# Two tables of half-block positions: the first head's steps and the last head's steps move by half a unit

## The chip, the cores and the metric

The kernel runs on one core of one Trainium2 chip. A core has a matrix engine (TensorE, PE in the rows; PEld are its weight loads), a vector engine (VectorE, DVE), an activation engine (ScalarE, ACT), a general engine (GpSimd, POOL) and a queue engine (SyncE, SP) that issues most transfers. The metric is the device time of one execution in microseconds, as the median of three runs.

## The reference

One layer of a decoder with four parallel branches, for 1024 prompt tokens and 8 x 4 sample tokens:

```python
h = rmsnorm(x, norm_g)
p = einsum('btd,dn->btn', h, w_in)        # one projection feeds all branches
o_a = silu(a_z) * (a_b * dwconv3(a_c * a_u))
o_r = silu(r_z) * head_norm(retention_chunked(rq, rk, r_v, S))      # 4 heads
o_c = silu(c_z) * silu(layernorm(dwconv31(glu)))
o_m = silu(m_z) * head_norm(sigmoid(m_o) * mlstm_chunked(q, k, v, i, f, C, n, m))   # 4 heads
proj = einsum('btnw,nwd->btnd', stack(o_a, o_r, o_c, o_m), w_br)
y = x + einsum('btd,de->bte', sum_n sigmoid(g_n) * proj_n, w_out)
```

Both kinds of heads work in chunks of 128 tokens: within a chunk by a masked product of q and k, between chunks by a state that is carried on. The results are the normalised outputs of the prompt and the sample, and the new states.

## The kernel before

Tokens lie along the free axis, channels on the partitions. Every large product is done in three parts (high x high, high x low, low x high), lines 1155 to 1157. The projection is cut into units of 128 output channels. A unit has three blocks of 352 tokens, a block two halves of 12 products each. There are 8 heads: heads 0 to 3 are mLSTM, heads 4 to 7 retention. While PE computes the units of the next head, the small matrix products of the head before are put between its halves.

The order is written out by a planner, `make_plan` (line 74). `phase` (line 78) lays out the halves of a group of units and puts the tasks of a table behind them: a task at position x comes after half x of the phase. `attention` (line 103) gives the 15 steps of a head: eight steps over the prompt's chunks, in which step c does the output of chunk c-1 (`b`) and the transposes and scores of chunk c (`a`); then the last chunk's output with the sample tokens' start (`as`); the sample tokens' products with the first state update (`bs1`) and the head's statistics (`pn`); the second state update (`bs2`); the normalisation (`pr`); an empty step; and the transposes back, first the prompt (`pt 0`), then the sample (`pt 1`). Each engine walks through the same list and does its own part of each entry, in that order, with waits on semaphores.

The places that matter here:

- `a` on PE, lines 1291 to 1312: L1308, L1309 and L1311 transpose k, v and o, L1312 is the score product. For the first head it waits until the gates are done (L2379 on DVE). ACT then makes kw (L1585), the sigmoid of o (L1597) and v (L1598), DVE the weighted scores sw (L2401).
- `b` on PE, L1327 to L1331, needs sw and v.
- `bs1` on PE, L1343 to L1354, ends with the first four state products (L1353, L1354); `bs2` is L1353 and L1354 again and needs DVE's first update (L2438) done.
- `pn` on DVE: L2471, L2474. `pr`: ACT's square root (L1626), DVE's reciprocal and shift (L2480, L2482), ACT's and DVE's scaling (L1629, L2487).
- `pt`: L1367 and L1371 on PE; L1371 waits until DVE has used the first of L1367's two results (L2498).
- In the last head's phase the units are cv, cg, z of that head, and two gate units (positions 0 to 29). The z unit's blocks are evicted by ACT (L1508) and DVE (L2022). Beside the head's steps the phase holds sums for the next stage (`comb`, `comb_split`, `comb4`: L2212, L1689, L1841, and the t4f operations L2224 to L2228, which need the result of L1841).
- The next stage is made of products of 264 tokens (L1204 to L1206). Its P7 product needs DVE's sum (L2073), behind the t4f operations and the first convolution taps (L1715, L2511) in DVE's queue.

Of the kernel before, what the change touches and what calls it, by code (L numbers as in the profile page):

```python
# [73 lines left out]
def make_plan():  # L74
# [3 lines left out]
    def phase(group, tasks):  # L78

        first, at = len(units), 0  # L80
        units.extend(group)
        blocks = [(u, b) for u in range(first, len(units)) for b in range(3)]
        if not first:

            blocks[:9] = [(u, b) for b in range(3) for u in range(3)]
        for u, b in blocks:
            for half in range(2):
                plan.append(("blk", u, b, half))
                if b == 2 and half:
                    plan.append(("unit_end", u))  # L90
                plan.extend(tasks.pop(at, ()))
                at += 1
        for more in sorted(tasks):
            plan.extend(tasks[more])

    def spread(steps, start, stride):

        out = {}
        for i, s in enumerate(steps):
            out.setdefault(int(start + i * stride), []).extend(s)  # L100
        return out

    def attention(hd):
        t = [[("a", hd, 0)]]
        t += [[("b", hd, c - 1), ("a", hd, c)] for c in range(1, CH)]
        t += [[("b", hd, CH - 1), ("as", hd)], [("bs1", hd), ("pn", hd)], [("bs2", hd)],
              [("pr", hd)], [], [("pt", hd, 0)], [("pt", hd, 1)]]
        return t

    def cols(base, h):  # L110
        return ("wa", (base + h * P) // P)

    def mlstm(h):
        return [("mq", cols(5632, h), h), ("mk", cols(6144, h), h), ("mv", cols(6656, h), h), ("mo", cols(7168, h), h)]
# [4 lines left out]
    def z(hd):  # L119
        return [("z", cols(7680, hd) if hd < 4 else cols(3584, hd - 4), hd)]  # L120

    def late(group, late_unit):

        return group[:2] + late_unit + group[2:]
# [8 lines left out]
    phase([("if", ("wi", 0), 0)] + mlstm(0)[:2] + z(0) + mlstm(0)[2:], gates)  # L133
    for h in range(1, 4):
        if h == 1:
            phase(mlstm(1), {x: step for x, step in zip((1, 3, 5, 6, 8, 9, 11, 12, 14, 15, 16, 17, 19, 21, 22), attention(0))})
        else:
            phase(late(mlstm(h), z(h - 1)), spread(attention(h - 1), 0, 2.05))
    for h in range(4):
# [10 lines left out]
        phase(late(ret(h), z(h + 3)), tasks)  # L150

    tasks = {}
    for x, step in zip((0, 1, 2, 4, 5, 6, 8, 9, 11, 13, 15, 16, 17, 18, 19), attention(7)):
        tasks.setdefault(x, []).extend(step)
    for i in range(6):
        tasks.setdefault(2 * i + 1, []).append(("comb", 3, i))
# [197 lines left out]
    for m in range(len(outs)):  # L354
        for b in range(3):
            plan_out.append(("pblk", m, b))
            x = 3 * m + b
# [16 lines left out]


UNITS, PAIRS, OUTS, SPL, LOADS, START, PLAN, SLOT_OF, PREV, AT_LOAD, AT_SPLIT, LAST_RING = make_plan()
NU, NW, NSPL = len(UNITS), len(PAIRS), len(SPL)
BRANCH_LAST = [8 * i + 7 for i in range(4)]
# [2359 lines left out]
```

How the kernel before makes its waits and increments, by code:

```python
        def loaded(eng, item):  # L920
            slot, n = LOADED[AT_LOAD[item]]
            eng.wait_ge(w_in[slot], 16 * n)
            return stage[slot]
# [1 line left out]
        def low_parts(eng, s):  # L926
            eng.wait_ge(lo_dve if by_vector(SPL[s]) else lo_done, LOW[s])
# [52 lines left out]
            def wait(self):  # L981
                self.eng.wait_ge(self.s, self.n)
# [2 lines left out]
        @block.sync  # L985
# [9 lines left out]
            def by_token(b):  # L995
                if b == 2:
                    sp.wait_ge(sq_done, 3)
                for j in range(3):
                    r0 = BLK * b + P * j
                    sp.dma_start(xk[b % 2][0:XCH[j], j, :], xtok[r0:r0 + XCH[j], :]).then_inc(xk_in[3 * b + j], 16)
# [14 lines left out]
            load(2, 0)  # L1016
            by_channel(3)
            by_token(2)
            by_channel(4)
            by_channel(5)
            sp.dma_start(vc[:, :, :], vec).then_inc(const_in, 16)
            sp.dma_start(m0t[:, :], m0).then_inc(const_in, 16)
            sp.dma_start(gb[:, :], gbias).then_inc(const_in, 16)
            load(3, 1)
            load(4, 2)
            sp.wait_ge(row_ready, 3)
            sp.dma_start(cst2[:, :], c2).then_inc(late_in, 16)
            def blk(u, b, half):
                if half and UNITS[u][0] == "g":
                    x = GN[(u, b)]
                    sp.wait_ge(freed["A"], FREED[("blk", u, b)][1])
                    sp.dma_start(g_rows[UNITS[u][2], :, tok(b)], gp[x % 2][:, :]).then_inc(gp_out[x % 2], 16)
# [52 lines left out]
        @block.tensor  # L1087
# [16 lines left out]
            pe.wait_ge(ones_set, 1)
            keep_busy(24)
```

## Time and profile before

| what | value |
|---|---|
| median of three runs | 1479.52 us (1478.79 to 1479.61) |
| the profiled execution | 1478.4 us |
| its span, first to last instruction | 1476.6 us |
| mean granted TensorE clock | 0.998 |
| PE busy | 1458.7 us (99%) |
| DVE, POOL, ACT busy | 914.5, 580.5, 520.1 us |

PE is the engine that sets the time. Busy time on the others matters where PE waits for them. The stretches of interest are the first head's first steps (about 95 to 102 us), its sample steps (137 to 140 us), the last head (570 to 592 us) and the start of the next stage (611 to 622 us). In a row of the timeline stand start, length, engine, line, operation, output and inputs, shapes, count, and in brackets the idle time before it with what ended it; start and length are in microseconds from the start of the span.

### The profile page before, as it was taken

The numbers are of one execution on the slowest core, as the hardware profiler recorded it, in microseconds if no ns is written. First come the engines' busy times: TensorE is split into PE (matmuls) and PEld (weight loads), VectorE is DVE, ScalarE is ACT, GpSimd is POOL, SyncE is SP. The second block draws the span as 40 slices with busy tenths as digits, with TensorE's granted clock in tenths as the row PEclk, the third lists the DMA queues.
The fourth block names the chain that finished last, engine by engine and source line by source line (L and its number), as shares of the span: only waits on it lengthen the run. The fifth ranks groups of instructions, "written<-read, shape, count | busy, mean of one in ns | idle before, by whom it ended". The sixth has DMA issues, their size and how long they took to land.

```text
span 1476.6 us, 26706 instructions
## 1 busy us (share of the span) xinstructions
PE 1458.7 (99%) x10318; PEld 1420.6 (96%) x10318; DVE 914.5 (62%) x1786; ACT 520.1 (35%) x1071; POOL 580.5 (39%) x456
## 2 busy tenths in 40 slices
PE   8999999999999999999999999999999999999998
PEld 8999999999999999999999999999999999999786
DVE  6455352556666665677977878867656324885542
ACT  6342333333334345333333342334454422220221
POOL 1000000000011021787777767776777844662100
PEclk9999999999999999999999999999999999999999
DMA  8120222212021121322223221222222476754222
GB/s 316 44 87 29 89 67 80 74 44 91 30 91 62 58 80 50 106 92 91 67 94 95 87 81 68 73 102 88 95 81 102 148 238 207 234 159 149 109 83 78
DMA packets 65527, 148.37 MB, mean 100 GB/s; under 512 B 7976, under 2 KB 36920, under 8 KB 65272
## 3 DMA queue, kind: packets, MB, share of 16 engines
q1 hardware_dynamic: 58008, 120.06, 24.3%
q0 software_dynamic: 6192, 22.27, 4.2%
q10 hardware_dynamic: 1200, 4.33, 0.7%
q8 instruction: 82, 1.34, 0.4%
q14 instruction: 45, 0.37, 0.1%
HBM read 110.99 MB, written 35.64 MB: 99 GB/s over the span
## 4 chain that ended last, share of the span: by engine, by line
PE 88%; DVE 5%; DMA 2%; POOL 2%; issue 1%; ACT 1%; SPq 0%; DVEq 0%; ACTq 0%; POOLq 0%
PE bank L1204 11%; PE bank L1206 11%; PE bank L1205 11%; PE bank L1155 9%; PE bank L1157 9%; PE bank L1156 9%; PE bank L1222 4%; PE bank L1223 4%; PE bank L1224 4%; PE bank L1416 1%; PE bank L1417 1%; PE bank L1418 1%; PE sums_ps L1312 1%; PE sums_ps L1327 1%; PE sums_ps L1331 1%
## 5 line engine op out<-in xcount | busy, mean ns | idle before, releaser
L1155 PE MATMUL bank<-h_hi,w_hi 128*128 128x352 f32 x960 | 319.4, 333 | 1.2 <-POOL w_lo L1802 1.0
L1157 PE MATMUL bank<-h_hi,w_lo 128*128 128x352 f32 x960 | 309.2, 322 | 0.0
L1156 PE MATMUL bank<-h_lo,w_hi 128*128 128x352 f32 x960 | 308.4, 321 | 0.0
L1204 PE MATMUL bank<-h_hi,t_hi 128*128 128x264 f32 x896 | 256.2, 286 | 0.0
L1205 PE MATMUL bank<-h_lo,t_hi 128*128 128x264 f32 x896 | 254.6, 284 | 0.0
L1206 PE MATMUL bank<-h_hi,t_lo 128*128 128x264 f32 x896 | 254.1, 284 | 0.0
L1802 POOL TENSOR_TENSOR t_lo<-stage,t_hi 128x512 fp32r<-128x512 f32 x144 | 194.7, 1355 | 139.5 <-ACT t_hi L1458 139.4
L1204 PE MATMUL bank<-c_hi,t_hi 128*128 128x264 f32 x672 | 191.3, 285 | 2.1 <-DVE part L2073 2.1
L1206 PE MATMUL bank<-c_hi,t_lo 128*128 128x264 f32 x672 | 191.0, 284 | 0.0
L1205 PE MATMUL bank<-c_lo,t_hi 128*128 128x264 f32 x672 | 190.3, 283 | 0.0
L1155 PEld LDWEIGHTS bank<-h_hi,w_hi 128*128 128x128 f32 x960 | 180.5, 188 | 2.9 <-POOL w_lo L1802 1.3
L1156 PEld LDWEIGHTS bank<-h_lo,w_hi 128*128 128x128 f32 x960 | 181.1, 189 | 0.0
L1157 PEld LDWEIGHTS bank<-h_hi,w_lo 128*128 128x128 f32 x960 | 180.3, 188 | 0.0
L1458 ACT ACTIVATE t_hi<-stage 128x512 fp32r<-128x512 f32 x144 | 90.9, 632 | 225.0 <-PE bank L1224 103.4
L1204 PEld LDWEIGHTS bank<-h_hi,t_hi 128*128 128x128 f32 x896 | 168.4, 188 | 0.8 <-issue 0.2
L1205 PEld LDWEIGHTS bank<-h_lo,t_hi 128*128 128x128 f32 x896 | 168.5, 188 | 0.5
L1206 PEld LDWEIGHTS bank<-h_hi,t_lo 128*128 128x128 f32 x896 | 168.5, 188 | 0.0
L2511 DVE SCALAR_TENSOR_TENSOR sums_ps<-ext,vc,sums_ps 128x1024 f32<-128x1024 f32 x116 | 149.1, 1285 | 13.3 <-ACT sums_ps L1715 9.7
L1819 POOL DMA_DIRECT2D out_o_s<-smp x8 | 4.4, 555 | 385.3 <-DVEq L2440 385.3
L1802 POOL TENSOR_TENSOR t_lo<-wsum,t_hi 128x512 fp32r<-128x512 f32 x84 | 111.0, 1323 | 81.2 <-ACT t_hi L1458 81.1
L1204 PEld LDWEIGHTS bank<-c_hi,t_hi 128*128 128x128 f32 x672 | 126.3, 188 | 2.7 <-issue 2.6
L1206 PEld LDWEIGHTS bank<-c_hi,t_lo 128*128 128x128 f32 x672 | 126.4, 188 | 0.0
(369 smaller groups left out, 2879.2 us busy)
## 6 DMA issues: line engine op xcount, KB each, us to landing
stage<-in_wa SPq DMA_DIRECT2D x64, 512.0 KB, 3.3
piece<-g_rows SPq DMA_DIRECT2D x96, 176.0 KB, 2.7
stage<-in_wg SPq DMA_DIRECT2D x32, 512.0 KB, 3.5
g_rows<-sgt SPq DMA_DIRECT2D x120, 132.0 KB, 1.9
o_raw<-o_rows SPq DMA_DIRECT2D x16, 528.0 KB, 6.2
stage<-in_wb SPq DMA_DIRECT2D x32, 256.0 KB, 2.8
xt<-in_xT SPq DMA_DIRECT2D x6, 704.0 KB, 12.7
o_rows<-zs POOLq DMA_DIRECT2D x8, 528.0 KB, 3.0
```

The lines of the kernel that those rows point to most:

```text
L1155: pe.matmul(out, hi, h_hi[:, k, tok(b)], start=(k == 0), stop=False)
L1156: pe.matmul(out, hi, h_lo[:, k, tok(b)], start=False, stop=False)
L1157: mm = pe.matmul(out, lo, h_hi[:, k, tok(b)], start=False, stop=(k == KD - 1))
L1204: pe.matmul(out, hi, a_hi(k), start=(first and k == 0), stop=False, skip_group_check=True)
L1205: pe.matmul(out, hi, a_lo(k), start=False, stop=False, skip_group_check=True)
L1206: mm = pe.matmul(out, lo, a_hi(k), start=False, stop=(k == 3), skip_group_check=True)
L1222: pe.matmul(out, hi, o_hi[n][:, k, tok(b)], start=(k == 0), stop=False)
L1223: pe.matmul(out, hi, o_lo[n][:, k, tok(b)], start=False, stop=False)
L1224: mm = pe.matmul(out, lo, o_hi[n][:, k, tok(b)], start=False, stop=(k == 3))
L1458: act.activation(dst_of(item)[0], split_src(item), ACT.Copy).then_inc(hi_done, 1)
L1802: pool.tensor_tensor(lo, split_src(item), hi.bitcast(F32), ALU.subtract).then_inc(lo_done, 1)
L2511: own(dve.scalar_tensor_tensor(cc[g][:, 0:TP] if k == CW - 1 else conv_ps, ext[g % 2][:, k:k + TP], vc[:, g, V_CW + k:V_CW + k + 1], conv_ ...
```

## The change

Two tables of positions have other numbers, line 136 for head 0 and line 153 for head 7:

```diff
-            phase(mlstm(1), {x: step for x, step in zip((1, 3, 5, 6, 8, 9, 11, 12, 14, 15, 16, 17, 19, 21, 22), attention(0))})
+            phase(mlstm(1), {x: step for x, step in zip((2, 3, 5, 6, 8, 9, 10, 12, 14, 15, 16, 17, 19, 21, 22), attention(0))})
-    for x, step in zip((0, 1, 2, 4, 5, 6, 8, 9, 11, 13, 15, 16, 17, 18, 19), attention(7)):
+    for x, step in zip((0, 1, 2, 4, 5, 6, 8, 9, 10, 12, 13, 15, 16, 18, 20), attention(7)):
```

No instruction is added or removed on any engine. For head 0, step 1 goes from position 1 to 2 and step 7 from 11 to 10. For head 7, the step with `as` goes from 11 to 10, `bs1` and `pn` from 13 to 12, `bs2` from 15 to 13, `pr` from 16 to 15, the empty step from 17 to 16, and `pt 1` from 19 to 20; `pt 0` stays at 18. The order of SP's transfers is unchanged; on POOL two stores of the last head's states now stand ahead of one L1841.

The first place is on PE, at the start of head 0: bank0 and bank1 are the accumulators of the first two blocks of the next head's first unit, sums_ps holds the head's small results. Before:

```order
457 L1155 MATMUL bank0<-h_hi_49,w_hi0_52 128x352
458 L1156 MATMUL bank0<-h_lo_50,w_hi0_52 128x352
459 L1157 MATMUL bank0<-h_hi_49,w_lo0_54 128x352
460 L1308 MATMUL sums_ps<-cst_82,qkv0_91 128x128
461 L1309 MATMUL sums_ps<-cst_82,qkv0_91 128x128
462 L1311 MATMUL sums_ps<-cst_82,ob0_119 128x128
463 L1312 MATMUL sums_ps<-qkv0_91 128x128
464 L1155 MATMUL bank1<-h_hi_49,w_hi0_52 128x352
```

The same step on PE after the change:

```order
469 L1155 MATMUL bank1<-h_hi_49,w_hi0_52 128x352
470 L1156 MATMUL bank1<-h_lo_50,w_hi0_52 128x352
471 L1157 MATMUL bank1<-h_hi_49,w_lo0_54 128x352
472 L1308 MATMUL sums_ps<-cst_82,qkv0_91 128x128
473 L1309 MATMUL sums_ps<-cst_82,qkv0_91 128x128
474 L1311 MATMUL sums_ps<-cst_82,ob0_119 128x128
475 L1312 MATMUL sums_ps<-qkv0_91 128x128
476 L1155 MATMUL bank1<-h_hi_49,w_hi0_52 128x352
```

The four small products moved behind the first 12 products of the second block, into its middle.

The second place is on DVE, in the last head: rt are the head's outputs, smp the sample states, stat and mv the statistics, zs the z product (bank0, bank1 its first and middle block). Before:

```order
631 L1936 TENSOR_TENSOR w_lo1_55<-stage1_57,w_hi1_53 128x1024
632 L2022 TENSOR_TENSOR zs_95<-bank0,sg0_99 128x352
633 L2445 TENSOR_TENSOR rt_98<-t1_109,sums_ps 32x128
634 L2438 SCALAR_TENSOR_TENSOR smp_97<-smp_97,cst_82,sums_ps 128x128 x4
635 L2471 BN_STATS stat_114<-rt_98 128x6 x9
636 L2474 BN_AGGR mv_115<-stat_114 128x2 x9
637 L2022 TENSOR_TENSOR zs_95<-bank1,sg1_100 128x352
638 L2438 SCALAR_TENSOR_TENSOR smp_97<-smp_97,cst_82,sums_ps 128x128 x4
639 L2480 RECIPROCAL rstd_116<-rstd_116 128x9
```

The same stretch of DVE after the change:

```order
631 L1936 TENSOR_TENSOR w_lo1_55<-stage1_57,w_hi1_53 128x1024
632 L2445 TENSOR_TENSOR rt_98<-t1_109,sums_ps 32x128
633 L2438 SCALAR_TENSOR_TENSOR smp_97<-smp_97,cst_82,sums_ps 128x128 x4
634 L2471 BN_STATS stat_114<-rt_98 128x6 x9
635 L2474 BN_AGGR mv_115<-stat_114 128x2 x9
636 L2022 TENSOR_TENSOR zs_95<-bank0,sg0_99 128x352
637 L2438 SCALAR_TENSOR_TENSOR smp_97<-smp_97,cst_82,sums_ps 128x128 x4
638 L2022 TENSOR_TENSOR zs_95<-bank1,sg1_100 128x352
639 L2480 RECIPROCAL rstd_116<-rstd_116 128x9
```

The first update and the statistics moved ahead of the first z product, the second update ahead of the middle one; the reciprocal has only the middle z product directly in front of it now.

The third place is on PE, at the last transpose of the last head: bank3 and bank4 are the first two blocks of the first gate unit. Before:

```order
3332 L1155 MATMUL bank3<-h_hi_49,w_hi1_53 128x352
3333 L1156 MATMUL bank3<-h_lo_50,w_hi1_53 128x352
3334 L1157 MATMUL bank3<-h_hi_49,w_lo1_55 128x352
3335 L1371 MATMUL sums_ps<-cst_82,rt_98 128x32
3336 L1155 MATMUL bank4<-h_hi_49,w_hi1_53 128x352
```

The same transpose on PE after the change:

```order
3344 L1155 MATMUL bank4<-h_hi_49,w_hi1_53 128x352
3345 L1156 MATMUL bank4<-h_lo_50,w_hi1_53 128x352
3346 L1157 MATMUL bank4<-h_hi_49,w_lo1_55 128x352
3347 L1371 MATMUL sums_ps<-cst_82,rt_98 128x32
3348 L1155 MATMUL bank4<-h_hi_49,w_hi1_53 128x352
```

The transpose moved behind the first 12 products of bank4's block.

## Rows read from the trace of the kernel before

**Rows 1.** The page's first line.

```profile
span 1476.6 us, 26706 instructions
```

**Rows 2.** PE's waits, whole span: us in total, times, longest us.

```profile
PE bank L1204 <- DVE part L2073: 2.1, 3, 1.1
PE sums_ps L1371 <- DVEq L2500: 1.9, 1, 1.9
...
PE sums_ps L1308 <- DVEq L2379: 1.3, 1, 1.3
```

**Rows 3.** Timeline of PE, 95 to 102 us, first head's first two steps.

```profile
95.35 0.32 PE L1157 MATMUL bank<-h_hi,w_lo 128*128 128x352 f32 x1
96.94 0.30 PE L1308 MATMUL sums_ps<-cst,qkv 128*128 128x128 f32 x1 [1.26 <-DVEq L2379]
...
97.43 0.41 PE L1155 MATMUL bank<-h_hi,w_hi 128*128 128x352 f32 x1
...
101.33 0.38 PE L1327 MATMUL sums_ps<-v,sw 128*128 128x129 f32 x2
```

**Rows 4.** Timeline of ACT and DVE, 97 to 101 us.

```profile
98.10 1.28 ACT L1597 ACT_TABLE_LOAD   x1
...
100.03 0.29 DVE L2401 TENSOR_TENSOR sw<-sums_ps,wt 128x128 f32<-128x128 f32 x1 [1.78 <-ACTq L1600]
```

**Rows 5.** Timeline of DVE and PE, 137 to 140 us, first head's state updates.

```profile
137.93 1.12 DVE L2438 SCALAR_TENSOR_TENSOR smp<-smp,decs,sums_ps 128x129 f32<-128x129 f32 x4
...
138.71 0.32 PE L1157 MATMUL bank<-h_hi,w_lo 128*128 128x352 f32 x1
...
139.16 0.45 PE L1353 MATMUL sums_ps<-vx,k 96*128 96x390 f32 x1
```

**Rows 6.** Timeline of PE, 577 to 592 us, last head.

```profile
577.06 0.37 PE L1155 MATMUL bank<-h_hi,w_hi 128*128 128x352 f32 x1
...
580.97 0.34 PE L1353 MATMUL sums_ps<-vx,k 96*128 96x390 f32 x1
...
581.21 0.37 PE L1155 MATMUL bank<-h_hi,w_hi 128*128 128x352 f32 x1
...
589.69 0.32 PE L1157 MATMUL bank<-h_hi,w_lo 128*128 128x352 f32 x1
591.90 0.25 PE L1371 MATMUL sums_ps<-cst,rt 32*128 32x32 f32 x1 [1.88 <-DVEq L2500]
```

**Rows 7.** Stretch: length, busy PE, PEld, DVE, ACT, POOL, granted clock, DMA.

```profile
587.00:592.00 5.00, 3.12 (x23) 2.81 (x21) 2.48 (x4) 3.35 (x5) 1.30 (x1) 1.00 0.03 11
```

**Rows 8.** Chain of waits, 560 to 640 us: start, us, what.

```profile
584.71 1.67 ACT rt L1629 x4
...
601.38 0.72 DVE t4f L2224
...
621.30 0.36 PE bank L1204
```

**Rows 9.** Timeline of PE, 619 to 622 us, next stage's first wait.

```profile
619.89 0.28 PE L1206 MATMUL bank<-c_hi,t_lo 128*128 128x264 f32 x1
621.30 0.36 PE L1204 MATMUL bank<-c_hi,t_hi 128*128 128x264 f32 x1 [1.13 <-DVE part L2073]
```

**Rows 10.** Timeline of ACT, 575 to 585 us: middle z block, square root.

```profile
581.17 0.47 ACT L1508 ACTIVATE sg<-bank 128x352 f32<-128x352 f32 x1 [3.02 <-PE bank L1157]
...
582.95 0.31 ACT L1626 ACTIVATE rstd<-mv,sse 128x9 f32<-128x9 f32 x1
```

**Rows 11.** Timeline of DVE, 581 to 586 us.

```profile
582.26 0.52 DVE L2022 TENSOR_TENSOR zs<-bank,sg 128x352 f32<-128x352 f32 x1
582.93 1.12 DVE L2438 SCALAR_TENSOR_TENSOR smp<-smp,cst,sums_ps 128x128 f32<-128x128 f32 x4
584.20 0.22 DVE L2480 RECIPROCAL rstd<-rstd 128x9 f32<-128x9 f32 x1
```

**Rows 12.** The t4f tile's second operation: duration ns min/median/max, first and last start.

```profile
L2226 DVE TENSOR_TENSOR t4f<-h_hi,t4f x4: 708/1192/1687, 602.1 to 612.9; 128x528 f32<-128x528 f32 x4
```

## The prediction

> **What bounds the kernel now.** I read the page first: the span is 1476.6 us [rows 1], and TensorE (PE in the rows) is busy in nearly all of it. So I went to the table of what PE waits for; three of its rows bear on the places that the change touches [rows 2]. Only PE's own waits can give time back here; a step on another engine counts only where PE ends up waiting for it. The timeline then shows where each wait stands. One is ahead of the first step of the first head, at 96.94 us [rows 3]. One is ahead of the last transpose of the last head, at 591.90 [rows 6]. The longest of the three waits on L2073 is at 621.30, after the last head, in the first product of the next stage that needs VectorE's (DVE's) sum [rows 9]. The granted clock is 1.00 in the stretch that holds the second wait, though PE is busy for only 3.12 of its 5.00 us [rows 7], so no term below needs a correction for the clock.
>
> The chain of waits adds the point on which my forecast rests. From 584.71 to 621.30 it does not run through PE at all: in 29 pieces it goes from the last head's normalisation on ScalarE (ACT) to DVE's twelve t4f operations, from 601.38, and ends at the wait at 621.30 [rows 8]. PE has slack against that chain until 621.30. What PE gains before it is kept only as far as the chain moves too.
>
> **The change part by part.**
>
> Unit of length: a half block is 12 products. Two of them take 580.97 - 577.06 = 3.91 us [rows 6], so one takes 1.95, and a product follows another after 0.16.
>
> First head, first step, half a block later. Before, the last product starts at 95.35, the next slot would be 95.51, and the step starts at 96.94: 1.43 us lost [rows 3]. After, a half block fills that slot, and the step starts at 95.51 + 12 x 0.16 = 97.43, behind the signal that ended the wait. But only one half block now stands between this step and the next (both tables have 3 as their second entry). The step takes 97.43 - 96.94 = 0.49 [rows 3], so PE reaches the next step's L1327 at 97.43 + 0.49 + 1.95 = 99.87. That one needs sw. In the profile sw is late because ACT's first sigmoid brings a table load of 1.28 us behind kw [rows 4]: from the step's start to the end of sw it is 100.03 + 0.29 - 96.94 = 3.38 us [rows 3, 4]. For the wake-up I take 0.11, from the second state update of the first head: DVE ends at 137.93 + 1.12 = 139.05 and PE starts at 139.16 [rows 5]. So L1327 starts at 97.43 + 3.38 + 0.11 = 100.92, with a new wait of 1.05 us. Before, it started at 101.33 [rows 3]. Gain: 0.41 of the 1.43 us. Bounds: 1.46 if the table load were no obstacle, nothing if the chain after the step grew by 0.4; I take 0.41, since every link of it has its row.
>
> First head, seventh step, half a block sooner. Two gaps of one half block now stand in a row. The rows of PE's waits have nothing for L1327 anywhere in the profile, and single gaps exist in it already; nothing is gained and nothing lost. ACT's weight split, which stood ahead of that step's four operations, stands behind them. Between ends of -0.2 and +0.3 (the size of the wait in the next paragraph) I take 0.
>
> Last head, sample steps sooner. They leave PE's work as it is, but one half block instead of two stands between the two state updates. The first head has that distance today: there the product before the second update starts at 138.71, the slot would be 138.87, the update starts at 139.16: 0.29 us of waiting [rows 5]. I take that price. It falls on PE in a place where PE has slack, so by itself it costs nothing at the end. On GpSimd (POOL), two stores now stand ahead of one subtraction, c_lo; it is read only by the t4f operations that start at 601.38 [rows 8], and is hidden.
>
> Last head, last transpose half a block later. PE's last product starts at 589.69, the slot is 589.85, the transpose starts at 591.90: 2.05 us lost [rows 6]. After, PE comes to it at 589.85 + 1.95 + 0.29 = 592.09, when its signal is there. Locally PE gains 2.05 - 0.29 = 1.76, with the first head 2.17 us.
>
> What is late next: the wait at 621.30. PE's slot there is 619.89 + 0.12 = 620.01, so the wait costs 1.29 us today [rows 9]; PE will now be there at 617.84. So the time is set by how far the chain moves. Its unbroken part starts with ACT's normalisation at 584.71 [rows 8], which needs DVE's reciprocal at 584.20. That one stood behind DVE's second state update, which ends at 582.93 + 1.12 = 584.05 [rows 11]. The update is now out of the way, and the reciprocal waits for ACT's square root alone. ACT, though, does this root behind the sigmoid of the middle z block, at 581.17 [rows 10], and PE ends that block later than now: the second update is in front of it (581.21 - 580.97 = 0.24 [rows 6]) with its wait (0.29), in all 0.53. So the root moves from 582.95 to 583.48 and ends at 583.79 (0.31 long [rows 10]); the reciprocal starts near 583.9, 0.3 us sooner than now. "Statistics sooner" is worth 0.3 us on the path, not the two microseconds by which they move on DVE.
>
> **Sum.** 0.41 (PE and all that follows it runs that much ahead since the first head) and 0.3 (chain): 0.7 us. The wait at 621.30 grows from 1.29 to 2.17 + 1.29 - 0.71 = 2.75 us. The profiled execution took 1478.4 us (1.8 more than its span), so 1477.7; the median of the runs is 1479.52, 1.12 above it, and by that measure I predict 1478.8.
>
> **What the trace cannot settle.** The twelve t4f operations are in the chain, and their time depends on what POOL does beside them: L2226, with one shape and one count of elements, takes from 708 to 1687 ns, 0.98 us apart [rows 12]. POOL's last subtractions in that stretch follow PE's last blocks, which come 2.17 us sooner, while t4f comes 0.7 us sooner. Which of the operations meet is drawn anew. Bounds: two fewer slow ones (-2.0 us), two more (+2.0). I take no change, since the number of POOL operations in the stretch stays.
>
> The Trainium skill, SBUF — State Buffer, "Who interferes with whom", says that a VectorE instruction with two SBUF inputs and a GpSimd instruction that reads SBUF exclude each other, and that the later one waits for the whole of the other. The trace agrees that such an operation has two prices (708 and 1687 ns [rows 12]). By the page, operations that meet in the other order would cost the chain nothing; by the row, each further meeting would cost 0.98 us; the rivals below take the row.
>
> **Rivals.**
>
> A, the gain arrives. The chain shortens with PE because t4f escapes POOL. Each operation that escapes saves 0.98 us: two give 1478.8 - 2.0 = 1476.8, and PE's own limit is 2.17 + 1.29 = 3.46 us, 1476.1. For it: POOL's late subtractions come sooner. Against: then they meet earlier t4f operations.
>
> B, slower. The same mechanism the other way, at 601 to 616 us: POOL's operations that follow PE move onto t4f operations that run alone today. One further meeting costs 0.98 and outweighs the 0.7: 1479.8; two 1480.8. It decides from the first on. Against it: only some of the twelve run alone, and POOL has no new work.
>
> C, the change does not do what it says. If the reciprocal still finds DVE taken (the z product of the middle block stands ahead of it), the chain starts 0.53 later instead of 0.3 sooner: 0.53 - 0.41 = 0.1 slower, 1479.6. Against it: that product is 0.52 long [rows 11] and can start when the sigmoid ends, 1.3 us and more before the root does.
>
> **How the numbers follow.** Forecast 0.62 (its own range 1478.1 to 1479.5), A 0.13, B 0.15, C 0.10. The range from A with two operations to halfway between B's two cases: 1476.8 to 1480.3. A measurement of this kernel can tell about 0.2%, 3.0 us, from no change. Faster by more than that needs nearly all of A: 0.06. Slower by more needs four further meetings: 0.03. The rest, 0.91, is within.
>
> **What would show it.** Right: no wait of L1308 on DVE; a new wait of L1327 of about 1 us near 100.9; no wait of L1371; a short one of L1353 near 577; ACT's root no sooner than now (583.48 less 0.41), the reciprocal at about 583.5; and the longest wait of L1204 on L2073 at 2.5 to 2.8 us, at about 620.6. Wrong: if that wait is as short as now or gone, with the span 2 to 3 us shorter, the chain was not the limit; if L1327 does not wait, the table load was not.

## The result, and the profile after

The changed kernel takes 1485.33 us (median of 6 runs, 1484.49 to 1486.91); the kernel before takes 1479.01 in the runs beside it (6 runs, 1478.79 to 1479.61). The ratio is 1.0042 [1.0031, 1.0052], with the 95% interval in brackets: slower by 6.3 us, where I predicted 0.7 us faster. The profiled execution took 1485.9 us, with a span of 1484.1 against 1476.6 [rows 1], so the traces differ by 7.5 us. (A position of the two tables is half a block of 12 products; most of the moved steps go by one position and `bs2` by two. The title's "half a unit" is not what the tables do.)

PE's waits come first, as before (us in total, times, longest us):

```profile
PE bank L1204 <- DVE part L2073: 8.7, 3, 7.7
...
PE sums_ps L1327 <- ACTq L1600: 0.8, 1, 0.8
```

The waits of L1371 and L1308 [rows 2] are gone, and the new wait of L1327 is there, as predicted. But the wait on L2073 has grown from 1.1 to 7.7 us. The timeline of PE after shows each of the places:

```profile
97.75 0.27 PE L1308 MATMUL sums_ps<-cst,qkv 128*128 128x128 f32 x1
...
101.20 0.46 PE L1327 MATMUL sums_ps<-v,sw 128*128 128x129 f32 x2 [0.81 <-ACTq L1600]
...
576.80 0.32 PE L1157 MATMUL bank<-h_hi,w_lo 128*128 128x352 f32 x1
577.24 0.44 PE L1353 MATMUL sums_ps<-vx,k 96*128 96x390 f32 x1
...
591.80 0.32 PE L1157 MATMUL bank<-h_hi,w_lo 128*128 128x352 f32 x1
592.04 0.24 PE L1371 MATMUL sums_ps<-cst,rt 32*128 32x32 f32 x1
...
618.13 0.28 PE L1206 MATMUL bank<-c_hi,t_lo 128*128 128x264 f32 x1
626.12 0.56 PE L1204 MATMUL bank<-c_hi,t_hi 128*128 128x264 f32 x1 [7.72 <-DVE part L2073]
626.48 0.42 PE L1205 MATMUL bank<-c_lo,t_hi 128*128 128x264 f32 x1
626.70 0.42 PE L1206 MATMUL bank<-c_hi,t_lo 128*128 128x264 f32 x1
...
631.50 0.29 PE L1204 MATMUL bank<-h_hi,t_hi 128*128 128x264 f32 x1
```

PE is early where it was meant to be: its slot ahead of the long wait is at 618.13 + 0.12 = 618.25 (620.01 before, from [rows 9]). The product that waits then starts at 626.12 instead of 621.30, 4.82 us later. And the 24 products behind it follow each other at 0.22 us, not 0.12: they take 631.50 - 626.12 = 5.38 us. The next row tells why (columns as in [rows 7]):

```profile
622.00:626.00 4.00, 0.00 (x0) 0.00 (x0) 2.94 (x4) 2.34 (x4) 3.38 (x3) 0.50 0.00 0
626.00:630.00 4.00, 3.88 (x17) 3.91 (x18) 3.63 (x5) 0.63 (x1) 3.86 (x4) 0.50 0.00 0
```

The granted clock is 0.50, the 1.2 GHz level, after an idle stretch of 7.87 us. In the kernel before the same 24 products run from 621.30 [rows 9] to 624.30, 3.00 us, at a clock of 1.00:

```profile
622.00:626.00 4.00, 4.00 (x36) 4.00 (x35) 3.90 (x7) 0.00 (x0) 3.86 (x4) 1.00 0.00 0
624.30 0.28 PE L1204 MATMUL bank<-h_hi,t_hi 128*128 128x264 f32 x1
```

So 4.82 + 2.38 = 7.20 of the 7.5 us are two things: a late sum, and half a clock behind it.

The sum is late because of the t4f chain in front of it. The timeline of ACT, DVE and POOL after, from the normalisation on:

```profile
582.76 0.54 POOL L1821 DMA_DIRECT2D out_o_p<-cn  x1
583.33 1.33 POOL L1841 TENSOR_TENSOR c_lo<-c_raw,c_hi 128x528 fp32r<-128x528 f32 x1
583.46 0.30 ACT L1626 ACTIVATE rstd<-mv,sse 128x9 f32<-128x9 f32 x1
583.80 0.21 DVE L2480 RECIPROCAL rstd<-rstd 128x9 f32<-128x9 f32 x1 [1.09 <-ACT rstd L1626]
584.05 0.65 DVE L2482 SCALAR_TENSOR_TENSOR shift<-mv,rstd 128x9 f32<-128x9 f32 x1
...
601.47 0.71 DVE L2224 TENSOR_TENSOR t4f<-c_hi,c_lo 128x528 f32<-128x528 f32 x1 [8.33 <-POOL c_lo L1841]
602.22 1.86 DVE L2226 TENSOR_TENSOR t4f<-h_hi,t4f 128x528 f32<-128x528 f32 x1
...
609.70 0.46 ACT L1545 ACTIVATE gp<-bank 128x352 f32<-128x352 f32 x1 [3.11 <-PE bank L1157]
...
613.73 0.94 POOL L1870 DMA_DIRECT2D ext<-in_chist  x1
614.49 5.19 DVE L2224 TENSOR_TENSOR t4f<-c_hi,c_lo 128x528 f32<-128x528 f32 x1
614.67 0.55 POOL L1875 DMA_DIRECT2D ahist<-in_ah  x1
615.24 3.87 POOL L1847 TENSOR_TENSOR h_lo<-t4f,h_hi 128x528 fp32r<-128x528 f32 x3
```

One t4f operation takes 5.19 us. It starts while POOL issues two transfers and ends at 619.68, 0.57 us after three h_lo subtractions are through (615.24 + 3.87 = 619.11). In the kernel before the chain ended at 614.64 + 1.69 = 616.33. The transfers began within its last operation, and h_lo came behind it:

```profile
584.45 0.17 DVE L2482 SCALAR_TENSOR_TENSOR shift<-mv,rstd 128x9 f32<-128x9 f32 x1
...
611.47 0.47 ACT L1545 ACTIVATE gp<-bank 128x352 f32<-128x352 f32 x1 [3.35 <-PE bank L1157]
...
614.64 1.69 DVE L2228 TENSOR_TENSOR t4f<-t4f,h_lo 128x528 f32<-128x528 f32 x1
615.71 0.94 POOL L1870 DMA_DIRECT2D ext<-in_chist  x1
...
617.22 3.87 POOL L1847 TENSOR_TENSOR h_lo<-t4f,h_hi 128x528 fp32r<-128x528 f32 x3
```

ACT empties PE's last block (L1545) 1.77 us sooner (611.47 to 609.70). POOL's subtractions follow ACT, and the transfer issues behind them came 1.98 us sooner (615.71 to 613.73); t4f came no sooner (601.38 to 601.47). Of the twelve t4f operations six take 1.57 us or more in the trace before; after, six lie between 1.57 and 1.86, and one more at 5.19.

### The profile page after: what moved, and what is told of

Same layout as the page of the kernel before. It is cut to its first block, busy times and chain, and to the rows that moved or that the text cites. A ratio compares the mean times of both kernels' runs of the same rounds, so it can differ in the third digit from the quotient of the medians.

```text
span 1484.1 us, 26706 instructions
## 1 busy us (share of the span) xinstructions
PE 1463.0 (99%) x10318; PEld 1424.3 (96%) x10318; DVE 920.6 (62%) x1786; ACT 519.4 (35%) x1071; POOL 578.1 (39%) x456
## 4 chain that ended last, share of the span: by engine, by line
PE 87%; DVE 5%; POOL 2%; DMA 2%; ACT 2%; issue 1%; SPq 0%; DVEq 0%; ACTq 0%; POOLq 0%
PE bank L1204 11%; PE bank L1206 11%; PE bank L1205 11%; PE bank L1155 10%; PE bank L1157 9%; PE bank L1156 9%; PE bank L1222 4%; PE bank L1223 4%; PE bank L1224 4%; PE bank L1416 1%; PE bank L1418 1%; PE bank L1417 1%; DVE sums_ps L2511 1%; PE sums_ps L1312 1%; PE sums_ps L1345 1%
## 5 line engine op out<-in xcount | busy, mean ns | idle before, releaser
L1802 POOL TENSOR_TENSOR t_lo<-stage,t_hi 128x512 fp32r<-128x512 f32 x144 | 193.7, 1347 | 140.0 <-ACT t_hi L1458 139.9
L1802 POOL TENSOR_TENSOR t_lo<-wsum,t_hi 128x512 fp32r<-128x512 f32 x84 | 110.4, 1316 | 85.9 <-ACT t_hi L1458 85.8
L1205 PEld LDWEIGHTS bank<-c_lo,t_hi 128*128 128x128 f32 x672 | 127.5, 190 | 0.1
```

The source lines that it names most:

```text
L1205: pe.matmul(out, hi, a_lo(k), start=False, stop=False, skip_group_check=True)
L1802: pool.tensor_tensor(lo, split_src(item), hi.bitcast(F32), ALU.subtract).then_inc(lo_done, 1)
```

## The experiments

Each kernel was timed in 3 rounds beside the kernel before, but for e13, which ran once. The kernel before took 1479.7 to 1480.2 us there. Theory L: the held operation, and the clock behind it, cost the 6.3 us, because the transpose's gain brings POOL's work forward onto t4f. (In the first expectations it is called theory P.)

**Which part does it.** e1 is the first head's table alone, e3 the change with its last number put back from 20 to 19, e4 only that number in the kernel before:

```diff
 e4, line 153
-... zip((0, 1, 2, 4, 5, 6, 8, 9, 11, 13, 15, 16, 17, 18, 19), attention(7)):
+... zip((0, 1, 2, 4, 5, 6, 8, 9, 11, 13, 15, 16, 17, 18, 20), attention(7)):
 e3, line 153
+... zip((0, 1, 2, 4, 5, 6, 8, 9, 10, 12, 13, 15, 16, 18, 19), attention(7)):
```

> The kernel before with the first head's new table alone. Theory P and the prediction's first term: a wait of L1327 of about 1 us in place of that of L1308, PE 0.1 to 0.4 us ahead from then on, time 1478.5 to 1479.1, no measurable change. Rival F (the first head's part carries a loss of its own): over 1480.

> The changed kernel with pt 1 of the last head back at 19. Theory P: PE waits again for about 2 us at 592, has no lead at 611, h_lo starts after the last t4f operation, and the time is that of the kernel before within 1 us, 1478 to 1480. Rival S: 1484 to 1486, since the sample steps and statistics stay sooner.

> The kernel before, with pt 1 of the last head at position 20 instead of 19 and nothing else. Theory P: PE gains its 2 us at 592 and with that lead sets off the same meeting of h_lo and t4f, so 1483.5 to 1486.5 with a t4f operation of 4 us or more. Rival S: the transpose's gain is kept or waited away at 621, 1477 to 1479.

e1: 1479.12 us, ratio 0.9994 [0.9985, 1.0004]. e3: 1479.49, 0.9996 [0.9986, 1.0005]. e4: 1485.13, 1.0034 [1.0021, 1.0047]. The one moved transpose carries the loss nearly whole; the sample steps and the first head carry none that can be measured. DVE's timeline in e4 has the held operation again, with the statistics unmoved:

```profile
614.91 5.19 DVE L2224 TENSOR_TENSOR t4f<-c_hi,c_lo 128x528 f32<-128x528 f32 x1
```

In e3 PE has its wait of 1.7 us before L1371 back, and the one on L2073 is 1.4:

```profile
PE bank L1204 <- DVE part L2073: 2.3, 3, 1.4
PE sums_ps L1371 <- DVEq L2500: 1.7, 1, 1.7
```

So a wait of PE that looked like pure loss was what kept POOL behind t4f.

**Is it the meeting with POOL?** e5 holds POOL until the last t4f operation is done; e6 puts the two transfers behind the h_lo subtractions.

```diff
 e5, in POOL's t4
+                pool.wait_ge(t4_ready, 4)
                 pool.wait_ge(t4_hi, k + 1)
 e6
-    late_tasks = {0: [("hist", 1), ("ahist",)], 1: [("t4", k) for k in range(4)]}
+    late_tasks = {1: [("t4", k) for k in range(4)] + [("hist", 1), ("ahist",)]}
```

> The changed kernel, and POOL's h_lo subtractions (L1847) wait until all twelve t4f operations of DVE are done. Theory P (the loss is DVE's L2224 blocked for 4.5 us by three h_lo subtractions in a row, which PE's lead has moved onto the t4f operations; the long wait of PE then halves the clock): no t4f operation over 2 us, PE's first wait on L2073 falls from 7.7 to 2.5 to 3.5 us, the clock stays at 1.00, time 1477.5 to 1479.2. Rival D (POOL's transfer issues L1870 and L1875, not the subtractions, block DVE): the t4f operation at the issues stays at 4 us or more, time 1484 to 1486. Rival S (the sooner sample steps cost it by themselves): 1484 to 1486.

> The changed kernel, with POOL's two transfer issues (L1870, L1875) behind the four h_lo subtractions instead of ahead of them. Theory P (subtractions in a row on POOL keep DVE's two-input operation out): h_lo starts at about 613.8, L2224 or its neighbour is still held for 2 us or more, 1481 to 1485. Rival D (the issues hold it): no t4f operation over 2 us, 1478.5 to 1480.5.

e5: 1480.32 us (1478.64 to 1482.16), ratio 1.0002 [0.9993, 1.0012]. A wait added on POOL gives back 5.0 us (1485.33 - 1480.32; 6.0 by the distances from the kernel before beside each), and no t4f operation is over 1.84 us: the meeting is the cause. The time is 1.1 us above the range that I expected, since PE's wait on L2073 is still 3.25 us and the clock in the profiled run (1481.62) falls behind it, where I expected 1.00:

```profile
622.00:626.00 4.00, 4.00 (x20) 4.00 (x20) 3.22 (x4) 0.09 (x1) 3.86 (x4) 0.50 0.00 0
```

e6: 1483.93 us, ratio 1.003 [1.0018, 1.0042]. No operation is held for long; instead the two engines take turns, each at some 1.7 us (the first row counts three of POOL's):

```profile
615.38 5.29 POOL L1847 TENSOR_TENSOR h_lo<-t4f,h_hi 128x528 fp32r<-128x528 f32 x3
616.13 1.61 DVE L2224 TENSOR_TENSOR t4f<-c_hi,c_lo 128x528 f32<-128x528 f32 x1
617.78 1.72 DVE L2226 TENSOR_TENSOR t4f<-h_hi,t4f 128x528 f32<-128x528 f32 x1
619.53 1.70 DVE L2228 TENSOR_TENSOR t4f<-t4f,h_lo 128x528 f32<-128x528 f32 x1
```

Nine slow operations instead of six: 3 x 0.98 = 2.9 us, and the clock is 0.50 behind PE's wait here too. So with the transfers out of the way the kernel still loses 4.2 us of 6.3. Neither expectation came out whole: the time lies in theory P's range, but no operation is over 2 us, as rival D had it. The transfers alone are not the cause; with them ahead of h_lo the meeting took the form of one long hold, without them that of turns. (They now stand ahead of POOL's next subtraction t_lo, L1802, which ends at 626.06; DVE's first sum of L2073 ends at 626.03. PE starts at 626.19, so how much of the 4.2 us belongs to either is not shown.)

**What the clock costs.** e7 puts 64 small products on PE in the wait; e11 puts 60 full-size ones there, e12 24 of them beside e5's wait.

```diff
 e11 and e12 (there 24), ahead of the wait of P7
+                    if w == 0 and tp == 0:
+                        for _ in range(60):
+                            pe.matmul(bank[4][:, SBK:512], t_hi[SLOT_OF[tile]][:, 0:P], h_hi[:, 0, 0:512 - SBK], start=True, stop=True,
+                                      skip_group_check=True)
                     pe.wait_ge(u2_done, n)
```

> The changed kernel, with 64 small products by a block of zeros (32 x 32 x 128, added to bank 4, whose sums they leave as they are) on PE ahead of its long wait for L2073. Theory P: DVE's late L2224 and so the end of the wait stay where they are, but PE is not idle before it, the granted clock stays at 1.00 behind it, and the 24 products there are issued every 0.12 instead of 0.22 us: 2 to 2.6 us of the loss come back, 1482.5 to 1483.8. Rival: the half clock costs nothing at the end, since DVE's chain is late behind it too: 1484.5 to 1486.

> The changed kernel with 60 further full-size products (128x248, operands that P7 itself reads) on PE just ahead of the long wait on L2073; they write columns of a bank that nobody reads and change no result. They fill about 60 x 0.12 = 7 of the 7.9 us without a product. Theory L (a long op holds the t4f chain 4.8 us longer, and the clock at 0.50 after the idle time costs about 2.4 us more): the granted clock stays 1.00 from 618 to 634 us, the 24 products after the wait take 3.0 us instead of 5.4, the first of them starts at 626.1 as before, and the kernel takes 1485.3 - 2.4 = 1482.9 us. If the clock cost nothing: 1485.3. If the products push the start of P7 late: over 1485.3, and then the timeline shows them running past 626.1.

> The changed kernel with POOL held until the four t4f operations of L2228 are done, and 24 such full-size products ahead of the wait on L2073, which is 3.3 us there. Theory L: clock 1.00 from 618 to 634, no t4f operation over 1.85 us, and the time of the held kernel (1480.3) less what the half clock cost it (24 products in 5.4 instead of 3.0 us): 1477.9, thus nearer to the 1478.8 that the blind sum gave. If the clock is not what the held kernel still pays: 1480.3.

e7 missed what I expected by far: 1501.36 us, 1.0145. On PE's timeline its products (two records for each) run far past the wait, and the clock falls while they run:

```profile
618.80 21.60 PE L1176 MATMUL bank<-cst 32*32 32x128 f32 x122
```

```profile
618.00:622.00 4.00, 4.00 (x38) 3.74 (x37) 3.38 (x2) 0.50 (x1) 2.10 (x2) 1.00 0.09 24
622.00:626.00 4.00, 4.00 (x29) 3.44 (x27) 2.69 (x3) 2.59 (x5) 3.15 (x3) 0.71 0.00 0
626.00:630.00 4.00, 4.00 (x21) 3.14 (x20) 3.05 (x4) 0.63 (x1) 3.86 (x4) 0.50 0.00 0
```

It prices nothing; in it the clock fell to 0.50 while PE was busy with the small products. With the full-size ones in the same place it stayed at 1.00. (Against what I expected, the added products of e11 and e12 spoil part of the first output, so these two do not compute the whole function and serve for their times alone.) e11: 1483.41 us, 1.0024 [1.0014, 1.0034], with the held operation still there (5.33 us) and a clock of 1.00:

```profile
618.96 6.96 PE L1176 MATMUL bank<-h_hi,t_hi 128*128 128x248 f32 x60
626.49 0.39 PE L1207 MATMUL bank<-c_hi,t_hi 128*128 128x264 f32 x1 [0.57 <-DVE part L2076]
...
629.51 0.28 PE L1207 MATMUL bank<-h_hi,t_hi 128*128 128x264 f32 x1
```

The 24 products take 629.51 - 626.49 = 3.02 us instead of 5.38. Between the medians of after and e11 lie 1.9 us, and between their distances from the kernel before beside each of them 2.9 (6.3 and 3.4): that is the clock's share of the 6.3. e12: 1478.6 us (1478.43 to 1480.67), 0.9991 [0.9981, 1.0], 1.7 below e5 and 1.4 below the kernel before beside it (1479.97). With POOL kept off t4f and the clock kept up, the changed kernel takes about the time that I predicted for it, 1478.8, or a gain of 1.4 us where I predicted 0.7. Neither alone does.

**Where the 0.3 us of the statistics went.** e13 puts the first c_lo of the last head ahead of the two state stores again (position 12 instead of 14).

> The changed kernel with the first of the last head's c_lo tasks at position 12 instead of 14, so that POOL's c_lo stands ahead of the two state stores again, as before the change. Theory: c_lo beside DVE's shift (L2482) is what ate the 0.3 us by which the reciprocal came sooner. Then L2482 takes 0.17 us again instead of 0.65, ACT's scaling of rt starts 0.4 to 0.5 us sooner (about 584.3 instead of 584.79), and t4f's first operation starts 0.4 to 0.5 us sooner than 601.47. Rival: something else sets the start of t4f, and it stays at 601.4 to 601.5 though L2482 is short. The whole time is not expected to tell more than 0.5 us either way, unless the shift by 0.5 us changes which operation is held behind the two stores.

```profile
584.40 0.22 DVE L2480 RECIPROCAL rstd<-rstd 128x9 f32<-128x9 f32 x1 [1.09 <-ACT rstd L1626]
584.65 0.17 DVE L2482 SCALAR_TENSOR_TENSOR shift<-mv,rstd 128x9 f32<-128x9 f32 x1
...
601.58 0.71 DVE L2224 TENSOR_TENSOR t4f<-c_hi,c_lo 128x528 f32<-128x528 f32 x1 [8.32 <-POOL c_lo L1841]
...
615.10 5.28 DVE L2226 TENSOR_TENSOR t4f<-h_hi,t4f 128x528 f32<-128x528 f32 x1
```

The shift is 0.17 us long again. All rows of this trace stand 0.5 to 0.6 us later from the start on (reciprocal 584.40 against 583.80); from the reciprocal to t4f it is 17.18 us here and 17.67 in the changed kernel. The 0.5 us are the c_lo that lay beside the shift. They do not help: the kernel took 1485.43 in its one run, with another operation held for 5.28 us.

**Why five microseconds and not 1.7?** e14, e15 and e16 put something between POOL's transfer issues and h_lo: sixteen waits already fulfilled, a wait on PE's second P6 product, a wait on its first P5 product.

```diff
 e15, in POOL's t4 (e16: P5, 0; e14: 16 times pool.wait_ge(t4_hi, 1))
+                if k == 0:
+                    pool.wait_ge(blk_done, DONE[("prod", 0, P6, 1)])
                 pool.wait_ge(t4_hi, k + 1)
```

> The changed kernel with sixteen waits that are long fulfilled between POOL's two late transfer issues and its first h_lo subtraction, so that POOL does nothing for some tenths of a us there. It tells what holds the long t4f operation (5.19 us in the changed kernel, caught between the issues and three h_lo in a row). Theory G (POOL keeps DVE out only when its operations follow the issue without a gap): the operation that stands beside the issues ends in the gap, within about 1 us of its start; the three h_lo then alternate with the later t4f operations, no operation is over 1.9 us, and the time comes out as with the issues behind h_lo, 1483.9 us or a little less, since at most three more slow operations are met. Theory I (an operation that starts beside an issue is held until POOL's whole train is through, gap or no gap): an operation of 5 us or more as before, and 1485.3 us. If the gap is too short to be seen in the rows (under 0.1 us), nothing is told.

> The changed kernel with a wait on PE's second P6 product between POOL's two late transfer issues and its h_lo subtractions. That product is done near 615.5 us, the issues end at 615.22, so POOL pauses for about 0.3 us. Theory G (POOL keeps DVE out only when its operations follow the issues without a pause): the t4f operation that starts at 614.5 beside the issues takes 0.7 us, the two or three after it alternate with h_lo at about 1.7 us each, none is over 1.9 us; the t4f chain ends near 618.3 instead of 621.2, and the time is near 1482.5 us, 1 us or more below the kernel with the issues behind h_lo. Theory I (an operation that starts beside an issue is held until POOL's train is through): an operation of 4.5 us or more again and 1485.3 us. If the gap in POOL's rows is under 0.1 us, nothing is told.

> The same with the wait on the first P5 product, done near 617.0 us: POOL pauses for about 1.8 us. Theory G: the last three t4f operations take 0.7 us each except for the last, which may meet the first h_lo; the chain ends at 616.7 to 617.7, and the time is that of the kernel with POOL held until t4f is done, 1480.3 us (up to 1481.3). Theory I: an operation that started beside the issue lasts until the train is through, near 620.8, and the time is 1485.3 or more.

e14: 1486.03 us, 1.004 [1.0026, 1.0054]; POOL's rows show no pause (616.15 to 616.17) and DVE an operation of 5.28 us. By its own condition it tells nothing. e16: 1479.99 us, 1.0001 [0.9991, 1.001], as theory G had it: POOL pauses for 1.83 us, and the operation that starts beside an issue at 614.38 takes 0.71. So standing beside an issue does not by itself hold an operation, and theory I falls. e15: 1481.82 us, 1.0016 [1.0006, 1.0026], its runs spread from 1478.50 to 1484.78. The profiled one is the quickest of them; its DVE and POOL rows:

```profile
615.13 0.71 DVE L2228 TENSOR_TENSOR t4f<-h_hi,t4f 128x528 f32<-128x528 f32 x1
615.40 0.55 POOL L1877 DMA_DIRECT2D ahist<-in_ah  x1
615.87 0.71 DVE L2230 TENSOR_TENSOR t4f<-t4f,h_lo 128x528 f32<-128x528 f32 x1
615.97 5.60 POOL L1849 TENSOR_TENSOR h_lo<-t4f,h_hi 128x528 fp32r<-128x528 f32 x4
```

POOL pauses here for only 0.02 us, as in e13, and the operation stands where e13's stood (615.13 and 615.10); yet it takes 0.71 instead of 5.28. (No trace shows what e15's slower runs met.) So theory G in its plain form, "without a pause", is not shown either, as far as the rows can show a pause. The overlap of the rows does not explain the hold either: in the changed kernel the operation, at 0.71 us, would have been over at 615.20, before the first subtraction's row begins at 615.24. What stays open is what in POOL's hand-over from an issue to a subtraction shuts DVE out for a whole train.

**A version that beats both.** t4f's first operation waits for all twelve c_lo, behind POOL's queue; it does not use the twelfth. e8 (in the kernel before) and e9 (in the changed one) wait for eleven:

```diff
-                    dve.wait_ge(comb_lo, 12)
+                    dve.wait_ge(comb_lo, 11)
```

> The kernel before with the same edit (11 instead of 12). Theory P: without PE's lead only the wait of 1.3 us at 621 can be saved: 1477.8 to 1479.3. Rival (t4f's start is worth something by itself, or the new neighbours on POOL make it slower): under 1477 or over 1480.5.

> The changed kernel, and DVE's t4f operations wait for 11 instead of 12 of POOL's c_lo subtractions; they read only the second third, which is complete with the eleventh. Theory P (the chain over t4f sets the time, PE's lead is there to be had): t4f starts at about 593 instead of 601.5 and is over before h_lo comes, PE's wait on L2073 falls to about 1 us, the clock stays, and the time is 3 to 4 us under the kernel before: 1475.5 to 1477. Rival: another link (part, L1665, and the taps) ends no sooner, wait 2.5 us or more, 1478 to 1480.

e8: 1479.21 us, 0.9996 [0.9987, 1.0005]; an operation is held here too, for 5.54 us, and PE's wait on L2073 is only 0.75. e9: 1476.88 us (1476.09 to 1477.61), 0.998 [0.9971, 0.999], faster than both kernels. DVE's timeline in e9:

```profile
593.30 0.71 DVE L2224 TENSOR_TENSOR t4f<-c_hi,c_lo 128x528 f32<-128x528 f32 x1 [0.34 <-DVE zs L2498]
...
603.51 5.53 DVE L2226 TENSOR_TENSOR t4f<-h_hi,t4f 128x528 f32<-128x528 f32 x1
...
612.46 1.68 DVE L2228 TENSOR_TENSOR t4f<-t4f,h_lo 128x528 f32<-128x528 f32 x1
```

The chain starts 8 us sooner and ends at 614.14 although an operation is held here too, for 5.53 us behind another issue and four POOL operations in a row. PE waits 0.9 us. Now the change is worth what PE gains by it: e9 is 2.3 us below e8, and I had worked out 2.17.

## Why the prediction was wrong

**Right: the terms on PE.** From the first head's step to L1327 it is 101.20 - 97.75 = 3.45 us (3.49 predicted), so the table load does bound it. The second update starts 577.24 - 576.96 = 0.28 behind its slot (0.29). L1371 waits for nothing. PE comes to the wait on L2073 1.76 us sooner on the trace's clock, and its rows stand some 0.3 us later from the start on (the first head's slot is 97.75 - 1.95 = 95.80 against 95.51), so 2.1 (2.17). And the frame was right: not PE but the t4f chain sets the time at 621, which e9 shows from the other side.

**Wrong: "and is hidden".** I let POOL's c_lo pass as hidden because only t4f reads it. It does not wait for anybody, but it lies beside DVE: the shift took 0.65 instead of 0.17 us. The reciprocal did come 0.40 us sooner (584.20 [rows 11] to 583.80); ACT's scaling, at 584.71 before [rows 8], then started at 584.79, and t4f at 601.47. e13 shows it. This alone would have cost 0.5 us.

**Wrong, and decisive: "I take no change, since the number of POOL operations in the stretch stays".** The number of ordinary meetings did stay at six. But the step took 0.98 us per meeting as the only price, from operations between 708 and 1687 ns [rows 12], which were all that the trace before held. The mechanism of rival B was the right one (POOL's operations that follow PE move onto t4f operations that ran alone), and it was mis-sized twice: a single operation cost 5.19 - 0.71 = 4.48 us, and even with the transfers out of the way the three h_lo met three operations (e6). I had the data to see where they would meet: POOL's h_lo began at 617.22, 0.89 us behind t4f's end at 616.33, and I myself had moved PE, and POOL with it, by 2.17 us against 0.7. I counted POOL's operations "in the stretch" and did not ask which were just outside of it. The Trainium skill, SBUF — State Buffer, "Who interferes with whom", which I had weighed, has the later instruction wait for the whole of the other. The trace agrees for the turns of 1.7 us, but the held operation, whose row begins 0.75 us ahead of the first subtraction's, waited for three of them; the measurement decides.

**Wrong: "no term below needs a correction for the clock".** I read that off the wait before L1371, 2.05 us long with a clock of 1.00 [rows 7]. It says nothing of another wait. After 7.87 us without a product 24 products ran at the 1.2 GHz level, for 2.4 us more in the traces, 1.9 to 2.9 by e11's median. For the wait that I forecast, 2.75 us, the nearest trace is e15's, 2.84 us, and there the clock stayed at 1.00; in e5's it fell behind 3.25 us.

Rival A did not come by itself; e9 is its case with the chain moved out of the way. Rival C's condition (DVE taken when the root ends) did not arise.

In sum: 4.82 us from the late sum and 2.38 from the clock make 7.20 of the traces' 7.5. (The 4.82 hold the later start of the trace's rows, 0.3.) The remaining 0.3 us comes at 819.42, where PE waits another 0.2 us for DVE (L2084), a wait that the kernel before does not have. The medians differ by 6.3, as the two profiled executions lie 0.6 above and 0.6 below theirs.

## What to carry to other kernels

When a wait on the busiest engine is removed, ask which other engines pace themselves by it: here 1.9 us taken from PE sent POOL's last subtractions into a chain on DVE that had ended 0.89 us before them. List what stands just outside a critical stretch on the engine whose operations lengthen those in it, not only what is in it. And count the clock behind a wait: here a wait of 7.87 us on PE cost 2.4 us more than its length in the traces, since the 24 products behind it ran at a granted clock of 0.50. The remedy that worked was to start the chain sooner (one count in a semaphore wait), not to speed up PE.

## What the runs showed of the hardware that I had not expected

- A two-input DVE operation of 128x528 that takes 0.71 us alone and 1.56 to 1.86 in turn with POOL took 5.19 to 5.54 us in eight of the sixteen traces, each time next to a POOL transfer issue with three or four POOL operations behind it. POOL's own operations then ran unstretched (about 1.3 us each, against 1.75 in turn). An operation at the same place took 0.71 us in e5, e15 and e16.
- The granted clock fell to 0.50 after 7.87 us without products, and after 3.25 us in e5's profiled run; after 3.24 us in e16's it stayed at 1.00. The spread of both kernels' runs (1478.6 to 1482.2, and 1478.4 to 1481.1) is wider than e12's, where nine of ten lie within 0.6 us. In e5 the time goes with the mean granted clock of the run: 0.999 at 1478.64 and 1479.54 us, 0.998 at 1479.72 to 1480.61, 0.997 at 1481.62, 1481.69 and 1482.16.
- In e7, with PE busy throughout on products of 32x32 tiles, the granted clock was 0.71 and then 0.50; in e11, with products of 128x248 in the same place, it was 1.00 throughout.
